# A hybrid encoder layer on one core: the router of three token tiles moved into the last output tile, and the waits around it

## The chip, the cores and the metric

The kernel runs on one core of one Trainium2 chip. The time is the device time of one execution in microseconds (us). Runs of the kernel before took 639.74, 640.41 and 641.4 us; the median, 640.41, is what the prediction is measured against.

## The reference

One layer on 512 tokens of width 1024, all in fp32: a mixer with three branches, then a mixture of experts, then a last norm.

```python
h = rms_norm(x, norm_mix[l]);  proj = h @ w_in[l]          # 1024 x 5120, gates included
o_na = neighbourhood_attention(...); o_s5 = s5_bidirectional(...); o_xa = memory_cross_attention(...)
merged = gates0 * (o_na @ w_br_na) + gates1 * (o_s5 @ w_br_s5) + gates2 * (o_xa @ w_br_xa)
x = x + merged @ w_out[l]
h2 = rms_norm(x, norm_ffn[l])
x = x + hierarchical_moe(h2, ...)
return rms_norm(x, final_norm)

# hierarchical_moe
coarse = h @ w_coarse + b_coarse            # 4 groups: the best one is taken
fine = h @ w_fine + b_fine                  # 16 experts, 4 in each group
top_v, top_i = lax.top_k(fine_g, 2)         # two experts of the chosen group
w_top = softmax(top_v) * p_grp
a = silu(h @ w_gate[e]) * (h @ w_up[e]) * comb;  y = a @ w_down[e]   # 16 experts, width 256
```

The S5 branch turns its input matrices B into a block form (`ba`) that is transposed on TensorE before the scan.

## The kernel before

Five engines run one program each, joined by semaphores; the order of the work on each is written out by hand. A matmul in fp32 accuracy is three fast ones (`split`, L1532 to L1537): each operand is kept as a high part (a cast on ScalarE) and a low part (a subtraction on VectorE). SyncE issues the loads.

**The projection.** 53 chunks of weights of 512 KB (`load(c)`, `hi(c)` on ScalarE L560, `lo(c)` on VectorE L962), then 8 more for the output projection. VectorE splits two chunks ahead and does the small work of the branches between them: after chunks 6 and 7 each it makes one half of the forward B (`forward_b`, L1078 to L1083, two 512-wide results), and at chunk 8 it copies the turned memory values (`v_take(0)`, L1195). TensorE turns the second half of these values after chunk 8 (`turn_values(1)`, L1670) and can start that once `v_take(0)` is done. `turn_b` (L1607) follows after chunk 9.

**The output projection** runs by tiles of 128 tokens. A tile is eight parts (`out_part(n, c, ...)`, six 512-wide matmuls each; parts 0 to 3 make the left half of the row, 4 to 7 the right). VectorE adds the residual (x2, L1342), ScalarE squares it and takes the root, VectorE inverts that and writes h2 (L1350); GpSimd stores h2 and x2 to DRAM (L2118, L2122). TensorE turns x2 in eight transposes (`x2_turn`, L1814), ScalarE copies the result (`x2_take`, L811), and `logits(n)` (L1821) multiplies it by the 20 router columns. In the kernel before the order on TensorE is: tiles 0 and 1, turn 0, tile 2, turn 1, logits 0, tile 3, turn 2, logits 1, turn 3, logits 2, logits 3. For the last tile GpSimd forms x2 times the gain (L2132) and ScalarE scales it (L830).

**The router.** VectorE biases the logits of all four tiles (L1360), counts comparisons (L1365 to L1371) and marks the two chosen experts of each token (`selb`, L1381, semaphore `chosen`). TensorE turns that into places by triangular and all-ones matmuls (L1847 to L1852, `places`). VectorE builds one-hot rows for the first four experts (L1401), TensorE multiplies them with token numbers (L1859), VectorE makes the index list (L1408, `idx0`), and GpSimd gathers the rows of h2 (`gather`, L2148). Besides, GpSimd writes token number and weight of every choice to DRAM in eight indirect DMAs (L2163), reads the whole list back in four DMAs (L2171), and then, expert by expert, copies the weight column (`wcur`, L2175), gathers the tokens of the expert three further on, and adds the result of the expert before (`add_y`, L413). For expert 4 and later the gather uses the list read back.

**The experts.** 16 experts, three units of 1 MB of weights each (gate and up in two halves, then down), nine buffers (`eraw`), three split copies (`unit_hi` L799, `unit_lo` L1413). In step e TensorE does the first half of gate and up of expert e, turns the activations of expert e-1 (L1903), turns the tokens of expert e+1 (`tokens`, L1871), does the second half, and then the down matmuls of expert e-1. ScalarE takes these from PSUM banks 2 and 3 scaled by the token's weight (`y_take`, L855), and the next down matmuls wait for that.

```python
L1866  pe.wait_ge(sem(f"xg{slot}"), gathered)        # tokens: the gather has landed
L853   act.wait_ge(sem("wcur"), e)                   # y_take: the weight is there
L2169  pool.wait_ge(sem("scattered"), 16 * 8)        # before the list is read back
```

Of the kernel before, what the change touches and what calls it, by code (L numbers as in the profile page):

```python
# [19 lines left out]
P = 128  # L20
D = 1024
# [96 lines left out]
def build(nc, a, out):  # L118
# [134 lines left out]
    hot = at("hot", 190.5, NHOT * NT * P, BF16)  # L253
    slots = at("slots", 196.5, NHOT * P)
    slotsi = at("slotsi", 199.5, NHOT * P, I32)
    tokf, toki = at("tokf", 198.5, 2 * NT, BF16), at("toki", 198.625, 2 * NT, I32)
    idx0 = at("idx0", 199, NHOT, I32)
# [100 lines left out]

    def cmul(eng, link, o, x, y, t):
# [46 lines left out]
    def add_y(pool, e):  # L406

        pool.wait_ge(sem("y_a"), e + 1)
# [10 lines left out]
    H2_BANK = (4, 7)  # L419
    B_BANK = (4, 5, 7, 3)  # L420
# [9 lines left out]
    def _(sp):  # L430
# [38 lines left out]
        sp.dma_start(v(lbias, 0, [1, 4]), a["moe_b_coarse"].partition_broadcast(P)).then_inc(sem("lb_in"), 16)  # L469
        sp.dma_start(v(lbias, 4, [1, 16]), a["moe_b_fine"].partition_broadcast(P)).then_inc(sem("lb_in"), 16)  # L470
# [43 lines left out]

        sp.wait_ge(sem("out_k"), NT)
        load_unit(0, 2, 5)
# [3 lines left out]
        load_unit(1, 2, 6)  # L520
# [33 lines left out]
    def _(act):  # L554
# [9 lines left out]
        def roots(k, j, n):  # L564

            act.wait_ge(sem("squares"), k)
            act.activation(v(stat, 16 + j, [1, n]), v(stat, j, [1, n]), ACT.Sqrt, scale=0.25 / D,
                           bias=v(stat, 49, [1, 1])).then_inc(sem("roots"), 1)
# [232 lines left out]
        def square_x2(n):  # L801

            act.wait_ge(sem("x2"), n + 1)
            junk = v(h2, D * n, [1, D]) if n < NT - 1 else v(gfin, 0, [1, D])
            act.activation(junk, v(x_sb, D * n, [1, D]), ACT.Square,
                           accum_out=v(stat, n, [1, 1])).then_inc(sem("squares"), 1)

# [8 lines left out]
        for n in range(NT - 1):  # L816
            square_x2(n)
            roots(n + 4, n, 1)
            if n:
                for j in range(2):  # L820
                    x2_take(n - 1, j)
        for j in range(2):
            x2_take(NT - 2, j)
        square_x2(NT - 1)
# [24 lines left out]
        def y_take(e, odd):  # L849
# [3 lines left out]
            act.wait_ge(sem("wcur"), e)  # L853
            for b in range(2):
                ins = act.activation(v(ysb, 512 * b + (0 if odd else D), [1, 512]), pv(2 + b, 0, [1, 512]),  # L855
                                     ACT.Identity, scale=v(wcur, 0 if odd else 1, [1, 1]))
            ins.then_inc(sem("y_a"), 1)

        def step(e0, i=None):
# [8 lines left out]
            if not peeled or e < 15:  # L868
                if peeled and e == 0:
                    unit_hi(2, 2, 1, 2)  # L870
                xt_take(e + 1, 1 - odd)
# [22 lines left out]
            elif not peeled or 2 <= e < 15:  # L894
                y_take(e, odd)
# [37 lines left out]
    def _(dve):  # L933
# [11 lines left out]
        def inverse_root(k, j, n):  # L945

            quarter, half, inverse = (v(stat, o + j, [1, n]) for o in (8, 16, 32))
            dve.wait_ge(sem("squares"), k)
            dve.tensor_scalar(quarter, v(stat, j, [1, n]), 0.25 / D, EPS / 4, MUL, ADD)
# [316 lines left out]
        for c in range(C_OUT):  # L1266
# [70 lines left out]
        dve.wait_ge(sem("gf_in"), 16)  # L1337
        for n in range(NT):
            dve.wait_ge(sem("out_k"), n + 1)
            for half in range(2):  # L1340
                xs = v(x_sb, D * n + 512 * half, [1, 512])
                ins = dve.tensor_tensor(xs, pv(2 * (n % 2) + half, 0, [1, 512]), xs, ADD)  # L1342
            ins.then_inc(sem("x2"), 1)
            if n == NT - 1:
                dve.wait_ge(sem("x2_turned"), 2 * NT)
                dve.tensor_copy(v(x2T, SEQ * 4 + P * n, [SEQ, 4], [1, P]), pv(H2_BANK[1], 0, [P, 4], [1, P])).then_inc(
                    sem("x2_took"), 1)
            inverse_root(n + 4, n, 1)
            if n < NT - 1:
                dve.scalar_tensor_tensor(v(h2, D * n, [1, D]), v(x_sb, D * n, [1, D]), v(stat, 24 + n, [1, 1]),  # L1350
                                         v(gffb, 0, [1, D]), MUL, MUL).then_inc(sem("h2"), 1)
        dve.sem_inc(sem("last_root"), 1)

        dve.wait_ge(sem("lb_in"), 32)
        for n in range(NT):
            if n in (0, NT - 1):
                dve.wait_ge(sem("logits"), NT if n else NT - 1)
            ins = dve.scalar_tensor_tensor(v(rt, 20 * n, [1, 20]), pv(5 + n // 3, 20 * n, [1, 20]), v(stat, 24 + n, [1, 1]),  # L1360
                                           v(lbias, 0, [1, 20]), MUL, ADD)
        link(ins)
        for j in range(4):
            n = j + 1
            ins = dve.tensor_tensor(v(rt, 80 + j, [16, 20], [4, n]), v(rt, j, [4, 20], [0, n]),  # L1365
                                    v(rt, 0, [4, 20], [1, n]), ALU.is_gt)
            if n < 4:
                ins = dve.tensor_tensor(v(rt, 80 + 4 * n + j, [16, 20], [4, 4 - n]), v(rt, j, [4, 20], [0, 4 - n]),
                                        v(rt, n, [4, 20], [1, 4 - n]), ALU.is_ge)
        link(ins)  # L1370
        link(dve.tensor_reduce(v(rt, 400, [1, 80]), v(rt, 80, [4, 80], [1, 4]), AX.X, ADD))  # L1371
        for j in range(2):
            ins = dve.tensor_scalar(v(rt, 480 + 80 * j, [1, 80]), v(rt, 400, [1, 80]), float(j), None, ALU.is_equal)
        link(ins)
        m = [v(rt, 640 + 64 * j, [1, 64]) for j in range(2)]
        for j in range(2):
            ins = dve.tensor_tensor(v(rt, 640 + 64 * j, [16, NT], [4, 4], [1, 4]),
                                    v(rt, 480 + 80 * j + 4, [20, NT], [4, 4], [1, 4]),
                                    v(rt, 480, [20, NT], [1, 4], [0, 4]), MUL)
        link(ins)  # L1380
        done(dve.tensor_tensor(v(selb, 0, [1, 64]), m[0], m[1], ADD), "chosen")  # L1381
        for j in range(2):
            ins = dve.tensor_tensor(v(rt, 768 + 64 * j, [16, NT], [1, 16]), v(rt, 640 + 64 * j, [16, NT], [1, 16]),
                                    v(rt, 4, [20, NT], [1, 16]), MUL)
        ins2 = dve.tensor_reduce(v(rt, 908, [1, NT]), v(rt, 0, [20, NT], [1, 4]), AX.X, ALU.max)
        link(ins2)
        link(dve.tensor_reduce(v(rt, 896, [1, 8]), v(rt, 768, [16, 8], [1, 16]), AX.X, ADD))
# [849 lines left out]
```

## Time and profile before

| what | us |
|---|---|
| median of the runs shown | 640.41 |
| the profiled execution, its own time | 639.83 |
| its span, first to last instruction | 638.2 |
| TensorE matmuls, busy | 588.4 (92%) |
| VectorE, busy | 416.5 (65%) |
| ScalarE, busy | 324.3 (51%) |
| GpSimd, busy | 221.4 (35%) |
| mean granted TensorE clock | 0.965 |

The profile is of one execution. PE is TensorE (PEld its weight loads), DVE VectorE, ACT ScalarE, POOL GpSimd, SP SyncE. Its times are counted from the first instruction of the span. A busy share is an average over stages with different limits, so it does not say which engine sets the end of a stage; the windows and timelines of the stage do. The granted clock is a share of full speed: 1.00 is 2.4 GHz and 0.50 is 1.2 GHz.

### The profile page before, as it was taken

Reading aid. Unit: us, or ns where it says so; the run is one execution under the profiler, and the core shown is the slowest. Engines: PE = TensorE matmul, PEld = TensorE weight load, DVE = VectorE, ACT = ScalarE, POOL = GpSimd, SP = SyncE. Lnnn points to the kernel's source line nnn. Section 1 sums busy time; section 2 is a strip of 40 time slices with the busy share of each in tenths; the row PEclk is TensorE's granted clock in tenths of the full one; section 3 lists DMA queues with packets and bytes.
Section 4 is the critical chain, followed back from the end, with each engine's and each line's share of the span. In section 5 each row is a group of like instructions: output and inputs, shape, how many; then the busy total and the mean of one; then the engine's idle time right before and its main releaser. Section 6 shows DMA issues by size and latency. Waiting matters only on the chain.

```text
span 638.2 us, 8989 instructions
## 1 busy us (share of the span) xinstructions
PE 588.4 (92%) x3149; PEld 477.0 (75%) x3149; DVE 416.5 (65%) x744; ACT 324.3 (51%) x533; POOL 221.4 (35%) x235
## 2 busy tenths in 40 slices
PE   2899799999999999999999999997497999999992
PEld 2688688889877777777677888887376888888871
DVE  3977523695376664554842379324877899999967
ACT  5866133222344433553243326315175998998853
POOL 3507985995000810000000000023665345434930
PEclk9899899999999999999999999997597999999997
DMA  9994523420253222222322336973599999999355
GB/s 299 197 217 115 116 68 101 126 72 1 63 169 88 78 66 67 67 67 66 100 65 67 100 99 155 334 275 132 158 324 405 374 365 393 399 386 374 130 108 199
DMA packets 89232, 111.46 MB, mean 175 GB/s; under 512 B 19647, under 2 KB 66913, under 8 KB 89192
## 3 DMA queue, kind: packets, MB, share of 16 engines
q1 hardware_dynamic: 79128, 93.65, 45.2%
q0 software_dynamic: 7280, 15.12, 8.7%
q10 hardware_dynamic: 2784, 2.18, 1.2%
q8 instruction: 23, 0.38, 0.2%
q14 instruction: 17, 0.14, 0.1%
HBM read 102.08 MB, written 14.75 MB: 183 GB/s over the span
## 4 chain that ended last, share of the span: by engine, by line
PE 77%; DVE 7%; DMA 5%; issue 4%; SPq 2%; POOL 2%; ACT 1%; POOLq 0%; ACTq 0%; DVEq 0%
PE bank L1535 21%; PE bank L1537 20%; PE bank L1536 20%; PE bank L1716 2%; PE bank L1690 2%; PE bank L1703 2%; DMA acc_scratch<-ysb,idx 2%; PE bank L1871 2%; DMA tok_scratch<-pay,rowi 1%; PE bank L1821 1%; SPq L483 1%; PE bank L1651 1%; DVE w_lo L962 1%; POOL tok_scratch L2163 1%; PE bank L1655 1%
## 5 line engine op out<-in xcount | busy, mean ns | idle before, releaser
L962 DVE TENSOR_TENSOR w_lo<-raw,w_hi 128x1024 fp32r<-128x1024 f32 x55 | 73.2, 1331 | 110.0 <-ACT w_hi L560 109.5
L1535 PE MATMUL bank<-h_hi,w_hi 128*128 128x512 f32 x320 | 129.6, 405 | 0.3 <-DVE w_lo L962 0.3
L1537 PE MATMUL bank<-h_hi,w_lo 128*128 128x512 f32 x320 | 126.1, 394 | 0.0
L1536 PE MATMUL bank<-h_lo,w_hi 128*128 128x512 f32 x320 | 125.6, 393 | 0.0
L1413 DVE TENSOR_TENSOR e_lo<-eraw,e_hi 128x2048 fp32r<-128x2048 f32 x48 | 108.7, 2291 | 8.9 <-ACT e_hi L799 7.6
L799 ACT CAST e_hi<-eraw 128x2048 fp32r<-128x2048 f32 x48 | 91.8, 1915 | 10.6 <-PE bank L1537 6.4
L560 ACT CAST w_hi<-raw 128x1024 fp32r<-128x1024 f32 x55 | 57.6, 1047 | 33.8 <-PE bank L1537 33.6
L1535 PEld LDWEIGHTS bank<-h_hi,w_hi 128*128 128x128 f32 x320 | 61.0, 191 | 13.1 <-DVE w_lo L962 0.9
L1537 PEld LDWEIGHTS bank<-h_hi,w_lo 128*128 128x128 f32 x320 | 60.6, 189 | 13.4
L1536 PEld LDWEIGHTS bank<-h_lo,w_hi 128*128 128x128 f32 x320 | 61.0, 191 | 11.7
L2113 POOL TENSOR_TENSOR wcf<-wcf,prt 128x160 f32<-128x160 f32 x1 | 0.5, 458 | 194.9 <-DMA wcf<-in_moe_w_fine 194.9
L1535 PE MATMUL bank<-e_hi,xt_hi 128*128 128x512 f32 x128 | 52.7, 412 | 1.6 <-DVE e_lo L1413 1.0
L1536 PE MATMUL bank<-e_lo,xt_hi 128*128 128x512 f32 x128 | 51.0, 398 | 0.0
L1537 PE MATMUL bank<-e_hi,xt_lo 128*128 128x512 f32 x128 | 51.0, 398 | 0.0
L413 POOL DMA_INDIRECT acc_scratch<-ysb,idx x14 | 25.6, 1831 | 56.8 <-PE bank L1871 41.6
L659 ACT ACTIVATE gt<-bank,bgh 128x512 f32<-128x512 f32 x24 | 16.5, 689 | 43.5 <-PE bank L1537 43.5
L2148 POOL DMA_INDIRECT xg<-h_scratch,idx x16 | 30.1, 1881 | 11.5 <-DVE idx L1408 8.6
L673 ACT ACTIVATE pr<-ssb,soft 128x192 f32<-128x192 f32 (+1 forms) x32 | 15.2, 475 | 30.2 <-DVE soft L1223 30.2
L1535 PE MATMUL bank<-e_hi,at_hi 128*128 128x512 f32 x64 | 26.1, 407 | 4.7 <-ACT ysb L855 3.7
L1535 PEld LDWEIGHTS bank<-e_hi,xt_hi 128*128 128x128 f32 x128 | 24.8, 193 | 7.3 <-DVE e_lo L1413 1.0
L1537 PEld LDWEIGHTS bank<-e_hi,xt_lo 128*128 128x128 f32 x128 | 24.6, 193 | 5.4
L1536 PEld LDWEIGHTS bank<-e_lo,xt_hi 128*128 128x128 f32 x128 | 24.8, 194 | 4.7
(390 smaller groups left out, 1228.5 us busy)
## 6 DMA issues: line engine op xcount, KB each, us to landing
raw<-in_w_in SPq DMA_DIRECT2D x40, 512.0 KB, 3.9
eraw<-in_moe_w_gate SPq DMA_DIRECT2D x32, 512.0 KB
eraw<-in_moe_w_up SPq DMA_DIRECT2D x32, 512.0 KB
eraw<-in_moe_w_down SPq DMA_DIRECT2D x32, 512.0 KB
raw<-in_w_out SPq DMA_DIRECT2D x8, 512.0 KB, 3.8
x_sb<-in_x SPq DMA_DIRECT2D x4, 512.0 KB, 5.0
raw<-in_w_mem_kv SPq DMA_DIRECT2D x4, 512.0 KB, 9.8
raw<-in_w_br_na SPq DMA_DIRECT2D x4, 512.0 KB, 3.4
```

The costliest lines, as they stand in the source:

```text
L413: pool.indirect_dma_start(out=acc_dram, out_offset=bass.IndirectOffsetOnAxis(ap=v(idx, 2 * e, [1, 1]), axis=0), in_=v(ysb, D * (e % 2), [1 ...
L560: act.copy(v(dst, o, [1, 1024]), v(raw, 1024 * (c % RAW), [1, 1024])).then_inc(sem("w_hi_done"), 1)
L659: ins = act.activation(v(gt, SEQ * m, [1, SEQ]), pv(g % 2, 0, [1, SEQ]), ACT.Tanh, scale=0.5, bias=v(bgh, KD * branch + m, [1, 1]))
L673: ins = act.activation(v(pr, 512 * (p % 2) + 256 * j, [1, n]), src, ACT.Exp, bias=v(soft, so + 1, [1, 1]), accum_out=v(soft, so + 2, [1, 1]))
L799: act.copy(v(e_hi[dst], 0, [1, 2048]), v(eraw[j], 0, [1, 2048])).then_inc(sem("e_hi_done"), 1)
L962: dve.tensor_tensor(v(l_, o, [1, 1024]), v(raw, 1024 * (c % RAW), [1, 1024]), raw32(v(h_, o, [1, 1024])), SUB).then_inc(sem("w_lo_done"), 1)
L1413: dve.tensor_tensor(v(e_lo[dst], 0, [1, 2048]), v(eraw[j], 0, [1, 2048]), raw32(v(e_hi[dst], 0, [1, 2048])), SUB).then_inc(sem("e_lo_done" ...
L1535: pe.matmul(dst, w[0], x[0], start=first, stop=False)
L1536: pe.matmul(dst, w[0], x[1], start=False, stop=False)
L1537: return pe.matmul(dst, w[1], x[0], start=False, stop=last)
L1690: ins = pe.matmul(pv(2 + j, 0, [1, n]), x, y, start=True, stop=True)
L2148: pool.indirect_dma_start(out=v(xg, D * (e % 3), [1, D]), out_offset=None, in_=h2_dram, in_offset=bass.IndirectOffsetOnAxis(ap=rows, axis= ...
```

## The change

- `forward_b` runs after chunks 5 and 6, not 6 and 7.
- On TensorE, tile 3's parts are interleaved with the router: logits 0 before part 0; logits 1 and the turn of tile 2 after part 0; logits 2 after part 1; the left half of tile 3 is turned after part 5; its half of the logits and the places of the first three tiles follow part 6. The right half of tile 3 is added, squared, turned and multiplied after part 7. VectorE routes tiles 0 and 1 together, then tile 2, then tile 3; `place` and `one_hot` are done for three tiles and then for the last.
- TensorE multiplies all-ones constants (`warm`) in its waits: 18 matmuls of 512 columns around the last tile's router, 18 after the index lists, 2 after the first tokens. Their results are read by nobody.
- The gain of tile 3's h2 moves from GpSimd to VectorE in halves; GpSimd's iotas move ahead to the first quarter of tile 3.
- The router's sums that the lists don't need come after all four lists; the first unit's low part is made in two halves after them; the overflow flag gets its counts last.
- `y_take(1)`, the first expert's, copies unscaled; `y_first` scales it in place before the second expert's, and the first `add_y` waits for that.
- The first two units of expert 2 are loaded after parts 5 and 7, the third after the gathers of experts 1 and 2 have landed; ScalarE splits the first unit after part 5. The load of the final norm's gain goes behind the split of unit 2.

```diff
-    UNIT_KB = (98.5, 106.5, 58.5, 66.5, 74.5, 138.5, 146.5, 154.5, 162.5)
+    UNIT_KB = (98.5, 106.5, 58.5, 66.5, 74.5, 138.5, 196.5, 154.5, 162.5)
-    HLK = [10.5, 26.5, 114.5]
+    HLK = [114.5, 10.5, 26.5]
...
+    LOGIT_BANK = (5, 5, 1, 0)
...
+        sp.wait_ge(sem("last_out"), 3)
+        load_unit(0, 2, 5)
         sp.wait_ge(sem("out_k"), NT)
-        load_unit(0, 2, 5)
+        load_unit(1, 2, 6)
         sp.wait_ge(sem("h2_out"), 16 * (NT + 2))
         sp.wait_ge(sem("logits"), NT)
         sp.wait_ge(sem("xg1"), 16)
-        load_unit(1, 2, 6)
+        sp.wait_ge(sem("xg2"), 16)
...
+        square_last(0)
+        act.wait_ge(sem("last_out"), 3)
+        unit_hi(0, 0, 1, 0)
         x2_take(NT - 1, 0)
+        square_last(1)
         roots(NT + 3, NT - 1, 1)
-        unit_hi(0, 0, 1, 0)
...
+            plain = isinstance(e, int) and e == 1
+            if not plain:
+                act.wait_ge(sem("wcur"), e)
...
+        def y_first():
+            act.wait_ge(sem("y_a"), 1)
+            act.wait_ge(sem("wcur"), 1)
+            act.mul(v(ysb, 0, [1, D]), v(ysb, 0, [1, D]), v(wcur, 0, [1, 1])).then_inc(sem("y_first"), 1)
...
-            if c in (6, 7):
+            if c in (5, 6):
                 dve.wait_ge(sem("ct_ready"), 2)
-                forward_b(c - 6)
-            if c == 7:
+                forward_b(c - 5)
+            if c == 6:
                 dve.sem_inc(sem("ba_ready"), 1)
...
+        dve.wait_ge(sem("logits"), 2)
+        dve.wait_ge(sem("last_out"), 1)
+        route(0, 2)
+        dve.wait_ge(sem("last_out"), 2)
+        x2_add(NT - 1, 0).then_inc(sem("x2_half"), 1)
+        x2_gain(0)
+        dve.wait_ge(sem("logits"), 3)
+        route(2, 1)
+        dve.wait_ge(sem("iotas"), 1)
+        place(0, NT - 1)
+        for e in range(NHOT):
+            one_hot(e, 0, NT - 1)
+        dve.wait_ge(sem("out_k"), NT)
+        x2_add(NT - 1, 1).then_inc(sem("x2"), 1)
+        x2_gain(1)
...
+        inverse_root(NT + 3, NT - 1, 1)
         dve.sem_inc(sem("last_root"), 1)
...
+        dve.wait_ge(sem("logits"), NT)
+        route(NT - 1, 1)
+        place(NT - 1, 1)
+        for e in range(NHOT):
+            one_hot(e, NT - 1, 1).then_inc(sem("hot"), 1)
...
+        for e in range(NHOT):
+            slot_list(e)
...
+        dve.wait_ge(sem("e_hi_done"), 1)
+        first_lo(0)
+        first_lo(1).then_inc(sem("e_lo_done"), 1)
         dve.wait_ge(sem("route_exp"), 1)
...
+        def warm(b, n):
+
+            for _ in range(n):
+                pe.matmul(pv(b, 0, [1, 512]), v(onesb, 0, [1, P]), v(onesb, 0, [0, 4], [1, P]), start=True, stop=True)
...
+        for j in range(2):
+            logits(0, j)
+        for c in range(C_OUT, NCH):
+            out_part(NT - 1, c, False)
+            if c == C_OUT:
+                for j in range(2):
+                    logits(1, j)
+                for j in range(2):
+                    x2_turn(2, j)
+            if c == C_OUT + 1:
+                for j in range(2):
+                    logits(2, j)
+            if c == C_OUT + 5:
+                x2_turn(NT - 1, 0)
+            if c == C_OUT + 6:
+                logits(NT - 1, 0)
+                places(True)
+        warm(4, 3)
+        x2_turn(NT - 1, 1)
+        warm(4, 3)
+        logits(NT - 1, 1)
+        warm(4, 9)
+        places(False)
+        warm(4, 3)
         for e in range(NHOT):
-            pe.wait_ge(sem("hot"), e + 1)
...
+            slot_list(e)
+        counts()
+        warm(0, 18)
...
-        pe.wait_ge(sem("rows"), 1)
         tokens(0, 0, 16)
+        warm(0, 2)
...
-        pool.wait_ge(sem("x2"), NT)
-        pool.wait_ge(sem("gf_in"), 16)
-        pool.tensor_tensor(v(h2, D * n, [1, D]), v(x_sb, D * n, [1, D]), v(gffb, 0, [1, D]), MUL).then_inc(
-            sem("h2_g"), 1)
-        pool.wait_ge(sem("out_k"), NT)
+        pool.wait_ge(sem("last_out"), 1)
```

## Rows read from the trace of the kernel before

**Rows 1.** Windows: stretch; length; busy PE, PEld, DVE, ACT, POOL; clock; DMA share; GB/s
```profile
200.00:300.00 100.00, 99.31 (x548) 74.63 (x547) 54.61 (x157) 44.90 (x107) 15.26 (x24) 1.00 0.25 71
...
67.00:71.00 4.00, 0.37 (x2) 0.00 (x0) 3.81 (x7) 1.53 (x2) 3.69 (x12) 0.99 0.73 161
...
71.00:74.00 3.00, 2.76 (x8) 2.31 (x9) 1.56 (x3) 0.00 (x0) 2.77 (x9) 0.50 0.12 32
...
440.00:443.00 3.00, 2.94 (x14) 2.83 (x14) 0.27 (x3) 2.98 (x4) 1.60 (x5) 0.50 0.62 236
...
484.00:488.40 4.40, 0.80 (x4) 0.34 (x2) 2.81 (x2) 1.93 (x4) 2.86 (x3) 0.88 1.03 412
...
488.40:494.00 5.60, 5.54 (x13) 4.41 (x14) 3.13 (x3) 1.97 (x2) 4.65 (x3) 0.50 1.03 408
```

**Rows 2.** Timeline of TensorE, 60 to 79: start, duration, then the idle before
```profile
61.61 0.50 PE L1535 MATMUL bank<-h_hi,w_hi 128*128 128x512 f32 x1 [0.31 <-DVE w_lo L962]
...
66.98 0.39 PE L1537 MATMUL bank<-h_hi,w_lo 128*128 128x512 f32 x1
...
71.24 0.66 PE L1670 MATMUL bank<-ident,vt 128*128 128x128 f32 x2 [3.87 <-DVE vm L1195]
...
78.44 1.91 PE L1607 MATMUL bank<-ident,ba 128*128 128x128 f32 x16
```

**Rows 3.** Timeline of VectorE, 54 to 72
```profile
55.03 1.85 DVE L962 TENSOR_TENSOR w_lo<-raw,w_hi 128x1024 fp32r<-128x1024 f32 x1 [0.20 <-ACT w_hi L560]
...
59.59 1.96 DVE L962 TENSOR_TENSOR w_lo<-raw,w_hi 128x1024 fp32r<-128x1024 f32 x1 [2.72 <-ACT w_hi L560]
...
70.67 0.42 DVE L1195 COPY vm<-bank 128x256 f32<-128x256 f32 x1 [0.15 <-DVE ba L1083]
```

**Rows 4.** Timeline of TensorE, 434 to 500
```profile
434.27 1.03 PE L1814 MATMUL bank<-ident,x_sb 128*128 128x128 f32 x8
...
437.76 5.19 PE L1821 MATMUL bank<-wcf,x2T 128*128 128x20 f32 x32
...
455.78 1.94 PE L1871 MATMUL bank<-ident,xg 128*128 128x128 f32 x8 [2.90 <-DMA xg<-h_scratch,idx]
...
458.27 0.80 PE L1535 MATMUL bank<-e_hi,xt_hi 128*128 128x512 f32 x1 [0.55 <-DVE xt_lo L1419]
...
480.99 1.05 PE L1871 MATMUL bank<-ident,xg 128*128 128x128 f32 x8
...
488.46 0.76 PE L1535 MATMUL bank<-e_hi,at_hi 128*128 128x512 f32 x1 [3.66 <-ACT ysb L855]
...
496.91 1.05 PE L1871 MATMUL bank<-ident,xg 128*128 128x128 f32 x8
```

**Rows 5.** Timeline of VectorE, 434 to 500
```profile
448.74 0.16 DVE L1408 SCALAR_TENSOR_TENSOR idx<-bank,rt 128x1 int32<-128x1 f32 x1
...
454.99 0.16 DVE L1444 TENSOR_TENSOR pay<-pay,rt 128x4 f32<-128x4 f32 x1
...
458.98 4.48 DVE L1413 TENSOR_TENSOR e_lo<-eraw,e_hi 128x2048 fp32r<-128x2048 f32 x2
```

**Rows 6.** Timeline of GpSimd, 434 to 500
```profile
449.85 2.23 POOL L2148 DMA_INDIRECT xg<-h_scratch,idx  x1 [7.85 <-DVE idx L1408]
...
459.03 3.08 POOL L2163 DMA_INDIRECT tok_scratch<-pay,rowi  x1 [0.30 <-issue]
...
468.42 0.97 POOL L2163 DMA_INDIRECT tok_scratch<-pay,rowi  x1 [0.30 <-issue]
...
469.69 3.11 POOL L2148 DMA_INDIRECT xg<-h_scratch,idx  x1 [0.30 <-issue]
...
487.23 1.06 POOL L2148 DMA_INDIRECT xg<-h_scratch,idx  x1 [0.15 <-issue]
```

**Rows 7.** DMAs that write the h2 scratch, all four
```profile
DMA to landing us min/median/max: 3.0/3.5/4.6
```

**Rows 8.** DMA, 476 to 480 us, GpSimd's queue: packets, MB, share of engines
```profile
q0 software_dynamic: 148, 0.52, 32.1%
```

More of the change, by code:

```diff
@@ L406, in add_y @@
     def add_y(pool, e):
-        pool.wait_ge(sem("y_a"), e + 1)
+        if e == 0:
+            pool.wait_ge(sem("y_first"), 1)
+        else:
+            pool.wait_ge(sem("y_a"), e + 1)
         if e == 0:
@@ L894, in step @@
             elif not peeled or 2 <= e < 15:
+                if peeled and e == 2:
+                    y_first()
                 y_take(e, odd)
@@ new lines, in x2_gain @@
+        def x2_gain(half):
+            n, o = NT - 1, 512 * half
+            dve.wait_ge(sem("x2" if half else "x2_half"), NT if half else 1)
+            dve.tensor_tensor(v(h2, D * n + o, [1, 512]), v(x_sb, D * n + o, [1, 512]), v(gffb, o, [1, 512]),
+                              MUL).then_inc(sem("h2_g"), 1)
+        for n in range(NT - 1):
+            dve.wait_ge(sem("out_k"), n + 1)
+            x2_add(n, 0)
+            x2_add(n, 1).then_inc(sem("x2"), 1)
+            inverse_root(n + 4, n, 1)
+            dve.scalar_tensor_tensor(v(h2, D * n, [1, D]), v(x_sb, D * n, [1, D]), v(stat, 24 + n, [1, 1]),
+                                     v(gffb, 0, [1, D]), MUL, MUL).then_inc(sem("h2"), 1)
@@ new lines, in logits @@
+        def logits(n, j):
+            if n == 0 and j == 0:
+                pe.wait_ge(sem("wcf_g"), 1)
+            pe.wait_ge(sem("x2_took"), 2 * n + j + 1)
+            for k in range(4 * j, 4 * j + 4):
+                ins = pe.matmul(pv(LOGIT_BANK[n], 20 * n, [1, 20]), v(x2T, SEQ * k + P * n, [1, P]), v(wcf, 20 * k, [1, 20]),
+                                start=k == 0, stop=k == KD - 1)
+            if j:
+                ins.then_inc(sem("logits"), 1)
+        def warm(b, n):
+            for _ in range(n):
+                pe.matmul(pv(b, 0, [1, 512]), v(onesb, 0, [1, P]), v(onesb, 0, [0, 4], [1, P]), start=True, stop=True)
@@ new lines, in places @@
+        def places(first):
+            pe.wait_ge(sem("chosen"), 2 if first else 3)
+            if first:
+                pe.matmul(pv(6, 0, [1, 48]), v(upper, 0, [1, P]), v(selb, 0, [1, 48]), start=True, stop=False)
+                for q in range(1, NT - 1):
+                    ins = pe.matmul(pv(6, 16 * q, [1, 48 - 16 * q]), v(onesb, 0, [1, P]), v(selb, 0, [1, 48 - 16 * q]),
+                                    start=False, stop=q == NT - 2)
+                ins.then_inc(sem("places"), 1)
+                for q in range(NT - 1):
+                    pe.matmul(pv(1, 0, [1, 16]), v(onesb, 0, [1, P]), v(selb, 16 * q, [1, 16]), start=q == 0, stop=False)
+            else:
+                pe.matmul(pv(1, 0, [1, 16]), v(upper, 0, [1, P]), v(selb, 48, [1, 16]), start=False, stop=True).then_inc(
+                    sem("places"), 1)
@@ new lines, in counts, with slot_list @@
+        def counts():
+            for n in range(NT):
+                ins = pe.matmul(pv(6, 64, [1, 16]), v(onesb, 0, [1, P]), v(selb, 16 * n, [1, 16]),
+                                start=n == 0, stop=n == NT - 1)
+            ins.then_inc(sem("places"), 1)
+        def slot_list(e):
+            pe.wait_ge(sem("hot"), e + 1)
+            for n in range(NT):
+                ins = pe.matmul(pv(HOT_BANK[e], 0, [1, 2]), v(hot, P * (NT * e + n), [1, P]), v(tokf, 2 * n, [1, 2]),
+                                start=n == 0, stop=n == NT - 1)
+            ins.then_inc(sem("hot_used"), 1)
@@ L2152, in _ @@
         pool.wait_ge(sem("h2_out"), 16 * (NT + 2))
+        pool.wait_ge(sem("logits"), NT)
         for e in range(3):
```

254 lines of the change are left out of this document (120 added, 134 removed).

## The prediction

> **What bounds the kernel now.** Read the windows first [rows 1]. Between 200 and 300 us TensorE is busy 99.3 of 100 us at full granted clock (1.00, the 2.4 GHz level), and it looks the same from 100 to 434 and from 500 to 600: there the kernel is bound by TensorE, and a change is worth what it takes out of TensorE's own queue, in full. So look for the stretches where it is idle or at the lower level (0.50, 1.2 GHz). There are three. (a) 67 to 71 us: 0.37 us busy of 4, then clock 0.50 until 74 [rows 1]. (b) 434 to 463: the router between the last output tile and the first expert. (c) 484.8 to 488.5, then 0.50 until 494 [rows 1]. The change touches all three.
>
> For each one I read the timeline of TensorE, then that of the engine named as releaser. (a): a transpose at 71.24 waited 3.87 us for VectorE's copy of the turned values, L1195 [rows 2]; VectorE reached that copy at 70.67 after a row of work without a gap from 59.59, and had been idle 2.72 us just before it [rows 3]. (b): the last output tile ends at 434.4; transposes and narrow logits matmuls follow until 442.98, the last 32 of them taking 5.19 us, and though TensorE is busy, the clock is down at 440 [rows 1, 4]; the decision is on VectorE until 448.9, the first gather is issued at 449.85 and the tokens are turned at 455.78; the first wide matmul is at 458.27 [rows 4 to 6]. (c): expert 0's down result stays in its banks until ScalarE has its weight, and the next down matmul waits 3.66 us for that [rows 4]. The weights come from the end of a long chain on GpSimd: eight scatters to DRAM (last at 468.42), their landing, four loads back, and only then the weight copy and the gather for expert 4 at 487.23 [rows 6].
>
> **B back (chunks 6, 7 to 5, 6).** On VectorE the first half of `forward_b` moves ahead of the split of chunk 8, into the 2.72 us gap. The row of work starts at 56.88 (55.03 + 1.85) and not at 59.59 [rows 3], so `v_take(0)` ends 2.7 us earlier, near 68.4. The price is that chunk 8's low part is ready some 1.1 us later (62.6), so that chunk 8 starts 1.1 us after 61.61 [rows 2]; it takes 5.6 us and ends at 68.3, just as the values are taken. TensorE passes the transpose at 68.5 instead of 71.24: -2.7. Its idle time is then two pieces of about 1.2 and 0.2 us, not one of 3.87, so I expect the clock to stay up. The seven matmuls in 71.55 to 74.54 ran at 427 ns, against 227 in the rest: -1.4. Sum **-4.1**. Ends: -2.5 if the clock falls all the same, -5.3 if the stall goes altogether (3.87 + 1.4). What depends on it later: TensorE has no wait over 0.7 us from 78 to 434, and the S5 work on GpSimd that it uses at 149 starts from TensorE's own lags, after 5.6 us of waiting at 103, so it moves along; what is won at 78 should still be there at 434.
>
> **Router inside the last tile.** TensorE now does, before the last output chunk, both logits of tiles 1 and 2 (1.70 us each), the turn of tile 2 (0.87), half of tile 3's turn (0.44) and logits (0.85), and six tiny place matmuls (0.35): 5.9 us at full clock. ScalarE's first split of an expert unit (1.89 us, from 435.85) stands ahead of its copy of the half tile, and holds the half logits 0.7 us. So the last output chunk ends at 434.4 + 6.6 = 441.0. VectorE routes two tiles after chunk 2 (2.4 us), adds half of tile 3 and gains it (1.3), routes tile 2 (2.1), places and makes four 384-wide one-hots (2.3); it ends these at 441.95 and only then adds the second half. Behind that stand in a row: add 0.65, turn 0.45, copy 0.75, logits 0.85, routing of one tile 2.0, place through TensorE 0.8, four one-hots 0.7, list and index 0.5: idx of expert 0 at 448.7, against 448.9 before [rows 5]. The chain after the tile shrinks from 14.5 us to 7.7, and the tile grows by 6.6: nothing is won at the first index. Those of experts 1 to 3 come 1.5 to 4 us earlier. But the h2 store of tile 3, off the path before, is now last: the add at 442.6, the square and the root (444.5), the scaling (445.7), then a landing of 3.0 to 4.6 us [rows 7]. The first gather starts at 450 (449.6 to 451), before at 449.85. It no longer waits for a split on VectorE (2.23 us, where the following ones take 1.0 [rows 6]): tokens 1.0 us earlier.
>
> **Constants.** 18 wide matmuls up to places, 18 after the lists, 2 behind the tokens; at 0.227 us each they fit into the waits. If they hold the clock, the 12 first matmuls (458.27 to 463.1 at 427 ns) cost 2.4 less and the turn of the tokens 0.9 less (1.94 against 1.05 us [rows 4]): first expert 4 us ahead of before. Ends: 0 to 4.3.
>
> **What is late next.** TensorE then wants expert 3's tokens at about 477, before at 480.99 [rows 4]. That gather was issued at 469.69, behind the scatters, and its half megabyte moved between 476 and 480 [rows 8]. So tokens 3 can't be turned before 480: of the 4 us, 1.0 is left. **Weighted later**: ScalarE takes expert 0's result unscaled after its split of unit 8 (485.2), so the down matmuls of expert 1 start at 485.3 and not at 488.46. TensorE then comes to expert 4's tokens at 491.1. Their gather at 487.23 can't be moved by this edit, for its rows come out of the same loads. With the 5.9 us of the first gather (449.85 to its use at 455.78) it lands at 493. Before, the turn was at 496.91 [rows 4]: **-3.7**. The extra scaling (1024 wide, some 1.2 us of ScalarE, two 512-wide take 1.27) falls into ScalarE's idle 3.6 us before 494. Two idles of about 3 and 2 us on TensorE remain, and either may drop the clock; 3.66 us did, and cost 13 x 0.2 = 2.6 us [rows 1]. Before expert 4's tokens this is hidden, behind them it isn't: I take off 0.7. Sum of the router, constants and weights: **-3.0**. After that the loop is bound by TensorE at 9.3 us a step, and I see no load late: unit 6 is preloaded and the others had landed 5 us or more before use.
>
> The GpSimd chain is the pivot, and I cost its shift at zero: the payload weights are ready at 455.6 (before 455.14 [rows 5]), since the four small groups are earlier and the first unit's low split (2.3 us) now stands ahead of them; scatters start at about 456.3, before 456.4. Its ends: -2 (the loads of units start a gather later and with one unit less, so scatters land sooner than the 8.5 us after the last of them) and +5 (below). The final-norm broadcast, 0.5 MB, now goes into the full DMA stretch: 0 to +1.3. New addresses, the bias on another semaphore and the split square (two halves and one 1-wide) I cost at nothing: VectorE and ScalarE both wait for TensorE there.
>
> **A rule weighed.** A scatter issued at 459.03 took 3.08 us and others 0.97; it ends 0.9 us after the first of two low splits that run on VectorE from 458.98 [rows 5, 6]. So GpSimd's indirect DMAs wait while VectorE subtracts two SBUF tensors. The Trainium skill says this too (GPSIMD Engine Reference, Key points: GpSimd shares its SBUF interfaces with VectorE, with contention where VectorE has two SBUF inputs), and the trace agrees. It speaks against this change: see rival 1.
>
> **Rivals.**
> 1. GpSimd's chain comes later and takes the gain of the expert stage. For: TensorE starts 4 us earlier, so the splits of units 3 and 4 (465 to 470) fall on scatters 5 to 8, where before they fell behind them; one held pair cost 2.1 + 0.9 = 3.0 us [rows 6]. Against: two splits of before are spread otherwise, and the landing is bound by the loads. Tokens 4 at 496: expert stage -0.9, plus 0.9 for a turn at half clock: 0. Time 640.4 - 4.1 = 636.3.
> 2. The constants hold the queue. They are bf16 with all ones, and if the clock is down at 444, the nine before `places` take 3.84 us and not 2.04 and end at 449.0, when the choice is made at 446.8: every index 2.5 us later. Expert stage near -0.5: 635.8. For: the clock fell at 438 to 440 while TensorE was busy with transposes and narrow matmuls [rows 1, 4]. Against: these now stand between wide ones.
> 3. B back does little (GpSimd's products slow the moved work, or chunk 8 starves): -2 there; with -3.0: 635.4, with rival 1 638.4.
> 4. Slower. One mechanism: every scatter and gather is held by a VectorE operation with two SBUF inputs. First halves hold gathers 1 and 2 (+2), units 3 and 4 hold scatters (+3), and the landing of the last grows from 8.5 to 12 us by the broadcast and the queue (+3.5). Tokens 4 land at 501.5, +4.6 against 496.91, the turn and 12 matmuls at half clock +3.3: 640.4 - 4.1 + 7.9 = 644.2. It decides once the shift of GpSimd's chain is over 6 us.
>
> **How the numbers follow.** The profiled execution took 639.83 us (span 638.2); the median shown is 640.41, 0.58 higher. -4.1 and -3.0 give 632.7 for an execution like the profiled one and 633.3 for the median. Chances: forecast (631 to 635) 0.52; rival 1 0.24; rival 2 0.10; rival 3 0.08; rival 4 0.06. Likeliest 633.3. Range: down to -5.3 and -5.5 (629.6), up to rival 3 with part of 1 (638). 0.3% is 1.9 us, about what a measurement of this kernel tells from no change. Faster takes all of the forecast and nearly all of rivals 1 to 3: 0.89; same 0.07; slower 0.04.
>
> **What would show it.** (a) the transpose at 71.24 at 68.5, no clock under 1.00 between 67 and 74, and all until 434 shifted by 4. (b) output ends 6.6 us later in its own terms; first gather at the same distance from the end of tile 2 (29 us) as before; granted clock 1.00 at the first 12 expert matmuls. (c) no wait of a down matmul for ScalarE over 2 us; instead a wait of TensorE at the tokens of expert 3 and of expert 4 for the gather. The forecast is wrong if `v_take(0)` still comes 3 us behind TensorE, if constants are seen at 427 ns ahead of `places`, or if scatters begin later than 36 us after the end of tile 2 (420.8) or the weights' copies later than 65.

## The result, and the profile after

The changed kernel takes **653.64 us** (median of 4 runs, 652.28 to 655.06) where the kernel before takes 640.32 beside it. The ratio on record is 1.0197, 95% interval 1.0176 to 1.0219: slower by 13 us, where 7 less were forecast. The profiled execution took 654.25 us, its span is 652.5. Of all the runs below one counts as slow (660.43 us, of `late_add`), and the ratios leave it out.

Start with TensorE's timeline of the kernel after, in the stretches that [rows 2, 4] showed of before (start, duration, idle before it and what ended that):

```profile
63.35 0.50 PE L1606 MATMUL bank<-h_hi,w_hi 128*128 128x512 f32 x1 [1.54 <-DVE w_lo L999]
69.33 0.41 PE L1741 MATMUL bank<-ident,vt 128*128 128x128 f32 x2 [0.24 <-DVE vm L1232]
...
75.07 1.91 PE L1678 MATMUL bank<-ident,ba 128*128 128x128 f32 x16
...
451.74 1.16 PE L1990 MATMUL bank<-ident,xg 128*128 128x128 f32 x8 [1.52 <-DMA xg<-h_scratch,idx]
453.86 0.50 PE L1606 MATMUL bank<-e_hi,xt_hi 128*128 128x512 f32 x1 [0.53 <-DVE xt_lo L1485]
...
476.82 1.97 PE L1990 MATMUL bank<-ident,xg 128*128 128x128 f32 x8 [2.46 <-DMA xg<-h_scratch,idx]
482.34 0.47 PE L1606 MATMUL bank<-e_hi,at_hi 128*128 128x512 f32 x1 [0.26 <-ACT ysb L881]
490.46 1.16 PE L1990 MATMUL bank<-ident,xg 128*128 128x128 f32 x8 [2.20 <-DMA xg<-h_scratch,idx]
```

B's transposes stand at 75.07 and not at 78.44, the expert stage's down matmuls at 482.34 and not at 488.46, and the tokens of expert 4 at 490.46 and not at 496.91. So far TensorE is 6.45 us ahead, near what the forecast had for this point (-4.1 and -3.7). All of it is lost behind this point, and 14 us more. The windows from 489 to 600 us (columns as in [rows 1]), first of before, then of after:

```profile
489.00:600.00 111.00, 111.00 (x539) 92.94 (x538) 103.00 (x92) 97.42 (x105) 56.49 (x38) 0.98 1.00 368
```

```profile
489.00:600.00 111.00, 98.57 (x466) 81.67 (x467) 91.06 (x81) 85.44 (x93) 43.36 (x32) 0.97 0.97 333
```

The expert loop, full on TensorE before, now has 12 us of idle in 111, at nearly the same granted clock (0.98 and 0.97). Who waits for what in that stretch (total us, times, longest), of before and then of after:

```profile
POOL acc_scratch L413 <- PE bank L1871: 41.6, 9, 6.1
POOL acc_scratch L413 <- DMA acc_scratch<-ysb,idx: 10.8, 2, 5.9
```

```profile
POOL acc_scratch L420 <- DMA acc_scratch<-ysb,idx: 65.8, 10, 7.9
...
PE bank L1990 <- DMA xg<-h_scratch,idx: 13.2, 6, 3.6
...
ACT ysb L881 <- DMA acc_scratch<-ysb,idx: 5.5, 4, 2.6
```

The line `POOL acc_scratch` is `add_y`, the accumulating DMA of an expert's rows. By its code (L408 to L412) it waits for two things: for its rows (`y_a`, from ScalarE) and for the landing of the add before it (`y_acc`). In after it waits for the landing all ten times, TensorE waits for gathered rows and ScalarE for a free `ysb`. The nine waits of before must not be read as they stand: the turn of the tokens (L1871) is no condition of an add. The wait for it belongs to the next gather, and the view names it because it came last. The starts of the adds, shown below, tell more. The first one, at 489.13, has its landing at

```profile
DMA to landing us min/median/max: 8.2/8.2/8.2
```

so (8.23 unrounded) at 497.35; ScalarE has the second expert's rows at 497.08:

```profile
495.82 1.26 ACT L855 ACTIVATE ysb<-bank,wcur 128x512 f32<-128x512 f32 x2
```

The second add starts at 498.21, 0.85 us behind the landing, just as the adds of after do. Sorted in this way, six of the eleven adds that follow the first in before start behind a landing, and five behind their rows, which come at most 0.4 us after the landing. So in before two loops of the same length go round together: TensorE, busy all 111 us, and the chain of adds. In after the rows are ready 7 to 11 us before the landing.

The chain of work that ended last has 18% in `DMA acc_scratch<-ysb,idx` after, where it had 2%:

```profile
PE 55%; DMA 22%; DVE 8%; issue 5%; POOL 4%; ACT 3%; SPq 2%; POOLq 0%; ACTq 0%; DVEq 0%
```

That share alone is no sign of a loss: the profile of `b_back_5` below, a kernel that is faster than before, has 17%.

Now the adds on GpSimd one by one, before:

```profile
489.13 1.67 POOL L413 DMA_INDIRECT acc_scratch<-ysb,idx  x1 [0.84 <-ACT ysb L855]
...
498.21 1.59 POOL L413 DMA_INDIRECT acc_scratch<-ysb,idx  x1 [4.26 <-PE bank L1871]
...
507.34 2.20 POOL L413 DMA_INDIRECT acc_scratch<-ysb,idx  x1 [6.11 <-PE bank L1871]
```

and after:

```profile
489.18 2.00 POOL L420 DMA_INDIRECT acc_scratch<-ysb,idx  x1 [4.70 <-ACT ysb L888]
...
499.39 3.67 POOL L420 DMA_INDIRECT acc_scratch<-ysb,idx  x1 [6.78 <-DMA acc_scratch<-ysb,idx]
...
511.79 1.59 POOL L420 DMA_INDIRECT acc_scratch<-ysb,idx  x1 [7.29 <-DMA acc_scratch<-ysb,idx]
...
520.85 3.65 POOL L420 DMA_INDIRECT acc_scratch<-ysb,idx  x1 [6.04 <-DMA acc_scratch<-ysb,idx]
```

The first add stands at the same 489.1 in both, though everything else is earlier. From there the first eleven are in the mean 9.30 us apart before and 10.88 after. What holds the first one is L888, the multiply of `y_first`. ScalarE after:

```profile
481.11 1.09 ACT L881 ACTIVATE ysb<-bank 128x512 f32<-128x512 f32 x2
482.12 0.38 ACT L914 ACTIVATE act_t<-bank 128x256 f32<-128x256 f32 x1
482.40 1.91 ACT L809 CAST e_hi<-eraw 128x2048 fp32r<-128x2048 f32 x1
485.41 1.92 ACT L809 CAST e_hi<-eraw 128x2048 fp32r<-128x2048 f32 x1 [1.10 <-PE bank L1608]
487.22 1.15 ACT L888 ACTIVATE ysb<-ysb,wcur 128x1024 f32<-128x1024 f32 x1
488.27 1.25 ACT L881 ACTIVATE ysb<-bank,wcur 128x512 f32<-128x512 f32 x2
```

The weight is there at 481 and the unweighted rows at 482.2, but the multiply stands behind the tanh and two casts and ends at 488.4. By then the second expert's rows follow at once (488.27): TensorE is a whole expert ahead of the adds. Before, the rows of the two experts were 9 us apart.

### The profile page after: what moved, and what is told of

Its sections match the earlier page's. It is cut to its first block, busy times and chain, and to the rows that moved or that the text cites. A ratio compares the mean times of both kernels' runs of the same rounds, so it can differ in the third digit from the quotient of the medians.

```text
span 652.5 us, 9114 instructions
## 1 busy us (share of the span) xinstructions
PE 596.2 (91%) x3190; PEld 478.0 (73%) x3190; DVE 421.6 (65%) x779; ACT 326.6 (50%) x537; POOL 214.4 (33%) x234
## 4 chain that ended last, share of the span: by engine, by line
PE 55%; DMA 22%; DVE 8%; issue 5%; POOL 4%; ACT 3%; SPq 2%; POOLq 0%; ACTq 0%; DVEq 0%
DMA acc_scratch<-ysb,idx 18%; PE bank L1606 15%; PE bank L1608 14%; PE bank L1607 14%; PE bank L1787 2%; PE bank L1761 2%; PE bank L1774 2%; POOL tok_scratch L2279 2%; DVE w_lo L999 2%; DVE h_lo L1025 1%; DMA xg<-h_scratch,idx 1%; SPq L491 1%; PE bank L1722 1%; PE bank L1899 1%; PE bank L1726 1%
## 5 line engine op out<-in xcount | busy, mean ns | idle before, releaser
L999 DVE TENSOR_TENSOR w_lo<-raw,w_hi 128x1024 fp32r<-128x1024 f32 x55 | 71.4, 1299 | 107.7 <-ACT w_hi L570 107.0
L1479 DVE TENSOR_TENSOR e_lo<-eraw,e_hi 128x2048 fp32r<-128x2048 f32 x47 | 106.7, 2293 | 12.5 <-ACT e_hi L809 12.5
L420 POOL DMA_INDIRECT acc_scratch<-ysb,idx x14 | 35.5, 2536 | 77.6 <-DMA acc_scratch<-ysb,idx 72.8
L1990 PE MATMUL bank<-ident,xg 128*128 128x128 f32 x128 | 19.5, 299 | 17.2 <-DMA xg<-h_scratch,idx 17.2
L1990 PEld LDWEIGHTS bank<-ident,xg 128*128 128x128 f32 x128 | 16.8, 196 | 19.6 <-issue 14.8
```

The costliest lines, as they stand in the source:

```text
L420: pool.indirect_dma_start(out=acc_dram, out_offset=bass.IndirectOffsetOnAxis(ap=v(idx, 2 * e, [1, 1]), axis=0), in_=v(ysb, D * (e % 2), [1 ...
L999: dve.tensor_tensor(v(l_, o, [1, 1024]), v(raw, 1024 * (c % RAW), [1, 1024]), raw32(v(h_, o, [1, 1024])), SUB).then_inc(sem("w_lo_done"), 1)
L1479: dve.tensor_tensor(v(e_lo[dst], 0, [1, 2048]), v(eraw[j], 0, [1, 2048]), raw32(v(e_hi[dst], 0, [1, 2048])), SUB).then_inc(sem("e_lo_done" ...
L1990: ins = pe.transpose(pv(4 + j, P * k, [1, P]), v(xg, D * slot + 4 * j + k, [KD, P]), v(ident, 0, [1, P]))
```

## The experiments

**Theory 1**: the serial chain of adds is the loop's bound as soon as TensorE is ahead of it. A landing takes 8.2 us and its release 0.8, 9.0 in all against TensorE's 9.3, so the chain has 0.3 us to spare and can't catch up; gathers stand behind the adds on GpSimd and `ysb` has two buffers, so the lag comes back to TensorE. (The eleven landings of before from 489 us on are 8.4 us in the mean. With the release that is 9.2, and the estimate of what is to spare falls to 0.1.) **Rival 2**: the new places of the weights and the order of their loads make the transfers longer. **Rival 3**: the transfers, gathers too, are too long once TensorE is ahead. **Rival 4**: ScalarE's order of work.

**B back alone**, on the kernel before:

```
-            if c in (6, 7): ... forward_b(c - 6)
-            if c == 7:
+            if c in (5, 6): ... forward_b(c - 5)
+            if c == 6:
                 dve.sem_inc(sem("ba_ready"), 1)
```

> The kernel before with B's first half turned one chunk earlier, nothing else of the change. Theory 1 (the adds into the accumulator have become the bound of the expert loop: each waits for the landing of the one before it, because the first still starts at 489.2 us while TensorE is a whole expert ahead) and its rival 2 (the new places of the split weights and of unit buffer 6, with the new order of the unit loads, make every transfer of the loop longer) both expect 636.3 to 636.9 us, which is 3.5 to 4.1 below the kernel before, with the adds 9.3 us apart and released by TensorE. A time near 650 would say that an earlier start of the same loop is enough to upset it.

Measured 638.56 us, 0.9935 (0.9898 to 0.9972). Repeated with more rounds:

> B's first half one chunk earlier alone, once more and with more rounds, beside the next kernel. The prediction's term for it: 3.5 to 4.1 us below the kernel before, a ratio of 0.9936 to 0.9945. If the loop's chain of adds swallows an earlier start, less: 0.996 or more.

637.19 us, **0.9924** (0.9894 to 0.9955). The term of 4.1 us stands in the medians. What theory 1 expected beside it, adds 9.3 us apart and released by TensorE, did not come: in both traces all eleven adds after the first wait for a landing, and the adds are 9.83 us apart in `b_back` and 9.50 in `b_back_5`. So an add that waits for the landing before it is not yet a loss. The first add is at 484 there, and TensorE waits for a gather 3.3 and 0.4 us in all from 489 to 600. The one execution traced for `b_back` (640.91 us) did lose in the loop what it had won before it.

**The weights' edit undone** in the changed kernel:

```
-        if e == 0: pool.wait_ge(sem("y_first"), 1)
-        else: pool.wait_ge(sem("y_a"), e + 1)
+        pool.wait_ge(sem("y_a"), e + 1)
...
-            if not plain: act.wait_ge(sem("wcur"), e)
+            act.wait_ge(sem("wcur"), e)
```

> The changed kernel with one edit undone: the first expert's rows are weighted on their way out of PSUM again, and the first add waits for them there. Theory 1 expects the first add at 483 to 484 us instead of 489.2, the adds 9.3 us apart again and released by TensorE, TensorE without waits at the tokens, and 634 to 636.5 us. Rival 2 (addresses and load order) expects adds still 10 to 11 us apart and more than 645 us.

635.28 us, **0.9909** (0.9878 to 0.9939); first add at 483.43. The adds are 9.61 us apart, and all of them wait for a landing, where 9.3 and a release by TensorE were expected. The changed kernel without this one edit is faster than before, with the new addresses, load order and constants all in: rival 2 falls.

**The same edit alone**, on the kernel before:

> The kernel before with only the first expert's rows weighted later, router, addresses and loads as they were. Theory 1: the 3.66 us wait at 488.46 goes, TensorE runs up to 3.7 us ahead, the first add still starts at 489 or later, the second waits for its landing, and from there the adds are 10 to 11 us apart: 645 to 655 us. Rival 2: addresses and loads are those of before, so adds stay at 9.3 us and the time is 636 to 641 us.

654.14 us, **1.0197** (1.0157 to 1.0236). This one edit is enough for the whole loss: it costs 13 us in the kernel before and, from 0.9909 or 0.9933 (repeated below) to 1.0197, 17 to 18 in the changed one. Its waits from 489 to 600:

```profile
POOL acc_scratch L416 <- DMA acc_scratch<-ysb,idx: 58.8, 9, 7.5
...
PE bank L1883 <- DMA xg<-h_scratch,idx: 12.7, 9, 2.6
```

**A late first add without the separate multiply**:

```
         pool.wait_ge(sem("y_a"), e + 1)
+        if e == 0:
+            pool.wait_ge(sem("e_hi_done"), 11)
```

> The changed kernel with the first expert's rows weighted on their way out of PSUM as before (635.3 us in that form), and in addition the first add held on GpSimd until the eleventh unit's high part is made, at about 488 us; nothing else differs. Theory 1: TensorE is then ahead of the adds as in the changed kernel, every add waits for the landing before it with a period of 10 to 11 us, 648 to 656 us. Rival 4 (it is ScalarE's work order, the separate multiply in front of the second expert's rows, that upsets the loop): nothing of that is here, 635 to 638 us.

655.31 us (650.08 to 660.43), **1.0233** (1.0171 to 1.0295). The first add starts at 492.01, later than the 488 that was meant. ScalarE's order is that of the kernel with the edit undone; only an add is held, and the loop goes the same way:

```profile
492.01 3.00 POOL L419 DMA_INDIRECT acc_scratch<-ysb,idx  x1 [7.37 <-issue]
...
502.48 1.94 POOL L419 DMA_INDIRECT acc_scratch<-ysb,idx  x1 [6.04 <-DMA acc_scratch<-ysb,idx]
...
512.49 2.13 POOL L419 DMA_INDIRECT acc_scratch<-ysb,idx  x1 [6.63 <-DMA acc_scratch<-ysb,idx]
```

**The wait on the landing lifted** in the changed kernel, with its late first add. The adds go into two tensors in turn; the second is not read, so this kernel leaves seven experts' rows out of its output and only its time counts:

```
+        elif e >= 2: pool.wait_ge(sem(Y_ACC[e % 2]), 16 * (e // 2))
-        pool.indirect_dma_start(out=acc_dram, ...).then_inc(sem("y_acc"), 16)
+        pool.indirect_dma_start(out=acc2_dram if e % 2 else acc_dram, ...).then_inc(sem(Y_ACC[e % 2]), 16)
```

> The changed kernel with the experts' rows added into two tensors in turn (the second filled from x at about 195 us, in the mixer), so that an add waits for the last but one and not for the one before. The second tensor is not read: the rows of experts 1, 3, 5 and so on up to 13 are left out of the output. Theory 1 (the chain of adds, one waiting for the other's landing, is the bound of the loop): adds are 9.3 us apart, released by TensorE, and the time is 632 to 637 us. Rival 3 (the transfers themselves, gathers too, are too long once TensorE is ahead): TensorE still waits for the gathered rows, over 645 us.

634.64 us, **0.9880** (0.9858 to 0.9902). The first add is at 490.47 and TensorE as far ahead as in the changed kernel, but the second add follows after 3.7 us and the others come as their rows do, 0.8 us behind them (the view names TensorE's turn here too):

```profile
490.47 2.00 POOL L423 DMA_INDIRECT acc_scratch<-ysb,idx  x1 [4.70 <-ACT ysb L892]
...
494.21 1.59 POOL L423 DMA_INDIRECT acc_scratch<-ysb,idx  x1 [0.30 <-issue]
...
503.68 1.84 POOL L423 DMA_INDIRECT acc_scratch<-ysb,idx  x1 [4.41 <-PE bank L1994]
```

From 489 to 600 us TensorE waits for a gather once (2.1 us), and the adds land in 8.6 us at the median: rival 3 falls. By this ratio the changed kernel with the serial chain out of its way would take 0.988 x 640.32 = 632.6 us; 633.3 was forecast.

**Half of each unit's load left out**, from the tenth unit on, in the changed kernel (its first add is late too, and with half of the weights stale only its time counts):

> The changed kernel with half of each weight unit loaded from the tenth unit on; the other half keeps the values of an earlier expert, so the experts from the third on are wrong in half of their weights. Theory 1 with landings stretched by the loads beside them: the adds land in 6 to 8 us instead of 9.4 to 11.6, the period falls to TensorE's 9.3 us, 632 to 637 us. If the length of a landing lies in the add itself and in its being held on GpSimd, the adds stay 10 to 11 us apart and the time stays over 648 us.

635.47 us, 0.9897 (0.9868 to 0.9926, two runs). Landings of the adds from 489, 520 and 560 us on, count and median:

```profile
acc_scratch<-ysb,idx POOLq DMA_INDIRECT x4, 8.7
...
acc_scratch<-ysb,idx POOLq DMA_INDIRECT x5, 7.7
...
acc_scratch<-ysb,idx POOLq DMA_INDIRECT x4, 6.2
```

In the changed kernel itself the same three are:

```profile
acc_scratch<-ysb,idx POOLq DMA_INDIRECT x3, 9.4
...
acc_scratch<-ysb,idx POOLq DMA_INDIRECT x4, 10.3
...
acc_scratch<-ysb,idx POOLq DMA_INDIRECT x4, 9.8
```

So the loads beside it stretch a landing. With less of them the chain catches up: seven adds wait for a landing, and from 557 us on they wait for their rows again. The landings are not 6 to 8 us from the start, as expected, but fall to that.

**The separate multiply kept, but early**, right behind `y_take(1)`:

```
                 if peeled and e == 2:
                     y_take(1, True)
+                    y_first()
...
-                if peeled and e == 2:
-                    y_first()
                 y_take(e, odd)
```

> The changed kernel with the separate multiply of the first expert's rows kept, but placed right behind their way out of PSUM, ahead of the third expert's tanh, instead of behind the casts of two units. Theory 1: only the time of the first add counts; it starts at 483 to 484 us instead of 489.2 and the time is within 1.5 us of the kernel with the weights as before, some 6 us below the kernel before. Rival 4 (the separate multiply or the unweighted rows upset ScalarE's order): still 648 us or more.

635.71 us, **0.9932** (0.9906 to 0.9957), first add at 483.60. Beside it the weights as before, again:

> The changed kernel with the first expert's rows weighted on their way out of PSUM, once more and with more rounds, as the measure for the two beside it. First add at 483 to 484 us, 6 us below the kernel before, as in its first run.

636.23 us, 0.9933 (0.9910 to 0.9955). Rival 4 falls; the two forms can't be told apart, and both beat the kernel before and the changed one.

**Without the constants** (weights as before):

> The changed kernel with the first expert's rows weighted as before and without the constants that TensorE is fed in its waits (41 matmuls of ones left out; none of them is read). In the prediction's sum the constants carry the clock of the short matmuls and of the first expert's: first wide matmul of the first expert 1 to 2 us later and at the lower clock for a while, 1 to 3 us longer than the same kernel with the constants. If the chain of adds and not TensorE sets the end, as theory 1 says of the loop, part or all of this is hidden: 0 to 1 us.

638.47 us, 0.9956 (0.9935 to 0.9978), 2.2 us over the same kernel with them, intervals overlapping. The windows 436 to 456, without and then with:

```profile
436.00:456.00 20.00, 8.59 (x64) 6.82 (x64) 15.71 (x63) 7.79 (x10) 6.76 (x7) 0.70 0.59 208
```

```profile
436.00:456.00 20.00, 16.27 (x105) 9.45 (x106) 15.92 (x63) 8.23 (x11) 6.39 (x7) 1.00 0.59 202
```

The constants hold the clock at 1.00, as forecast; the turn of the first tokens takes 1.16 us with them and 1.97 without.

**Without B**, the weights as before and then with the early multiply:

> The changed kernel with the first expert's rows weighted as before and B's halves turned one chunk later, as before: the router part, the constants and the new places alone. By the prediction's sum B is worth 3.5 to 4 us: 638.8 to 639.5 us where the same kernel with B back took 635.3. If B's gain is lost in the loop, 635 to 637 us.

640.98 us, 0.9994 (0.9966 to 1.0023).

> The changed kernel with the separate multiply placed right behind the way out of PSUM, as in first_early, and with B's halves turned as before: router, constants and the early first add alone. The prediction's term for it: 3.0 us below the kernel before, a ratio of 0.995. Theory 1: the adds are 9.0 to 9.3 us apart at best and the first one starts only as much earlier as GpSimd's chain of scatters and index loads does, so what TensorE gains beyond that is lost again: 0 to 3 us, 0.995 to 1.0.

641.27 us, 0.9999 (0.9972 to 1.0026). The router part alone, forecast at -3.0, gives nothing that shows. On top of B it does no better: 0.9933 and 0.9932 with it, 0.9924 for B alone.

One table, each row from its own trace, counted from the first turn of output tile 0 (408.90 in before), which takes out what lies upstream. "Lead" is tokens of expert 4 minus first add; "apart" is the mean of the first ten distances of adds; "tail" runs to the end of the span.

| kernel | first add | lead | apart | tail | ratio |
|---|---|---|---|---|---|
| before | 80.2 | 7.8 | 9.30 | 229.3 | 1 |
| no_b | 78.7 | 5.7 | 9.07 | 226.7 | 0.9994 |
| early_no_b | 79.5 | 5.1 | 9.19 | 228.5 | 0.9999 |
| weights_as_before | 78.0 | 5.1 | 9.61 | 230.3 | 0.9909 |
| weights_as_before_5 | 79.4 | 6.7 | 9.16 | 229.2 | 0.9933 |
| first_early | 78.7 | 5.1 | 9.17 | 227.7 | 0.9932 |
| b_back | 79.2 | 5.7 | 9.83 | 234.4 | 0.9935 |
| b_back_5 | 77.7 | 5.1 | 9.50 | 230.2 | 0.9924 |
| no_warm | 80.4 | 5.7 | 9.54 | 232.7 | 0.9956 |
| after | 83.6 | 1.3 | 10.88 | 247.0 | 1.0197 |
| weights_later_alone | 82.2 | 1.7 | 10.93 | 243.9 | 1.0197 |
| late_add | 84.1 | -0.1 | 10.46 | 240.5 | 1.0233 |
| two_acc2 | 83.6 | 1.1 | 8.77 | 227.8 | 0.9880 |
| half_loads | 82.5 | -0.2 | 8.77 | 227.5 | 0.9897 |

The lead is the room that the chain has to fall behind before TensorE feels it. With the serial chain and full loads, a lead of 5 us or more goes with adds 9.1 to 9.8 us apart, one under 2 with 10.5 to 10.9. Where between the two it tips wasn't tried. In `two_acc2` and `half_loads` the adds are closer than TensorE's 9.3 us because they catch up.

## Why the prediction was wrong

**The sum was right up to its last row.** B back: -4.1 forecast; 3.4 earlier at B's transposes, 0.9924 alone. Half logits held by ScalarE: 0.7 forecast, 0.64 seen. Scatters from 453.21 on, 3.2 us earlier and so unmoved but for B, as costed. The transpose of (a) at 69.33 (68.5 forecast), the clock at 1.00 from 67 to 74. Tokens of expert 4: -7.8 forecast before 0.7 for the clock, -6.45 seen; some 3 us of variation upstream lie over it (see Open). The prediction's rivals 1 to 3 are no part of the loss. Splits of units 3 and 4 did fall on scatters 7 and 8 (2.14 and 1.89 us), but their landing took up what they cost.

**The step that failed** is one sentence: "After that the loop is bound by TensorE at 9.3 us a step". It was never priced against the second chain that goes round in this loop, add, landing, add. Both numbers were in the trace of before: landings of 8.3 us at the median, and six adds of eleven that start 0.85 us behind the landing of the one before. They say that the slack was 0.1 to 0.3 us a step: the chain of adds was as long as TensorE's loop already. TensorE 6.45 us ahead of a chain whose first link had not moved could gain nothing, at best 13 links of 9.3 us from the same 489.1. That alone makes a change of no effect of a change forecast at -7.

**The weights' edit was priced only on TensorE and ScalarE.** The prediction asks where the multiply fits on ScalarE ("ScalarE's idle 3.6 us before 494") and not who waits for it. It was the first add: from where it could go at 483.4 (weights_as_before) to 489.2. The edit is there to take a wait of 3.66 us from TensorE, and it puts 5.8 us on a chain with next to no slack. In the changed kernel it did not even save that wait. With the edit undone, TensorE has no such wait in `weights_as_before` and the tokens of expert 4 at 488.51, before the 490.46 of the changed kernel; in `weights_as_before_5` the wait is 2.17 us.

**And the late chain is also slower**: 10.88 us a link for 9.30. From the first add to the last it is 136.6 us, before 122.5; with a first add 3.4 us later in the kernel's own count that makes the longer tail (247.0 for 229.3). Two things stretch it. The issue on GpSimd takes 2.54 us in the mean, before 1.83. Adds whose issue overlaps none of VectorE's low splits take 1.6 us in both traces, and the one at 520.85, of 3.65 us, lies over these:

```profile
520.74 2.29 DVE L1479 TENSOR_TENSOR e_lo<-eraw,e_hi 128x2048 fp32r<-128x2048 f32 x1 [0.93 <-ACT e_hi L809]
523.20 2.38 DVE L1479 TENSOR_TENSOR e_lo<-eraw,e_hi 128x2048 fp32r<-128x2048 f32 x1 [0.16 <-ACT e_hi L809]
```

The rest is the transfer beside the unit loads: issue to landing is 9.9 us at the median, before 8.3, and falls to 6.2 in the last stretch of half_loads. How much of the 1.6 each has was not separated: the longer issue can account for 0.7 us of it at most, and that the loads matter half_loads shows. Why the late chain meets longer landings stays open. It isn't that each add waits for the one before: in `b_back_5` all of them do, with landings of 8.4 us at the median. Nor does a slow chain stay slow of itself: in `b_back` the first four links are 10.2 to 11.5 us and the later ones 8.7 to 9.9. The Trainium skill (GPSIMD Engine Reference, Key points) has GpSimd share its SBUF interfaces with VectorE; the trace agrees, and has it at the issue of an indirect DMA (3.65 us here, 1.59 for the add at 511.79, which overlaps no such subtraction). An overlap does not always stretch it: the add at 492.76 in `first_early` takes 1.59 us wholly beside a low split.

The prediction's rival 4, the slower side, had the hold of GpSimd's DMAs as a part, but put it in the router and behind a GpSimd chain 6 us late. That chain was not late; it was met from the other side, by a TensorE 6 us early. The mechanism was not among the rivals.

**Open**: the router part wins 2.6 and 0.8 us of tail in two traces without B and nothing in the medians (0.9994, 0.9999), while the kernels with B and an early first add are 3 to 6 us below before (0.9956 to 0.9909). The first turn of tile 0 stood between 408.90 and 412.1 us in traces of kernels that are the same up to there, so some 3 us of upstream variation lie over a term of 3. These times neither confirm nor refute the term. It fits that the chain of adds swallows it: with the chain lifted (two_acc2) the ratio is 0.9880 (0.9858 to 0.9902), 3 us under first_early's 0.9932 (0.9906 to 0.9957). But two accumulators on the kernel before weren't tried, so how much they give without the router part isn't known.

## What to carry to other kernels

When a stage is bound by one engine, look for the other loops that go round in it, and write down each one's period and slack: an engine moved ahead can only use the slack of the others. Price a deferred operation at everyone who waits for its result, above all at the first link of a serial chain, which sets the place of all later ones. A chain whose link is a DMA in a full DMA stretch has no fixed period: its links were 8.7 to 11.5 us long within one trace here. And check a named releaser against the code and the times before it carries an argument.

## What the runs showed of the hardware

An accumulating indirect DMA of 0.5 MB lands 8.3 us after issue at the median in before, 8.4 in b_back_5, 9.9 in after, and 6.2 beside half of the loads, once these have been gone for a while; the next one that waits for it starts 0.8 us later. The DMA engines are as busy in both (share 1.00 and 0.97 from 489 to 600 us) but move 368 GB/s before and 333 after: a full share doesn't say that DMA's throughput is the bound. Here the bound was the latency of single transfers, one behind the other, each stretched by the loads beside it.
